# Hybrid RWKV-7 / NSA decoder step: the compression stage takes the prompt's group first, with its rows loaded in the stage ahead

## The chip, the cores and the metric

One core of one Trainium2 chip runs the whole kernel. The metric is device time in microseconds (us), median of several executions. All matrix work of the stage around the change is in fp32; each fp32 product shows as two PE instructions in the trace.

## The reference, cut to what matters

One inference step of one layer, for a prompt of 1024 tokens and 8 sample sequences of 4 new tokens with 2048 past tokens each. The NSA half compresses keys and values: a convolution of width 32 and stride 16 over the tokens, a bias from a position table, gelu, and a second product.

```
def _compress(x, w1, pe, w2):
    b, n, g, dh = x.shape
    xt = jnp.swapaxes(x, 1, 2).reshape(b * g, n, dh)
    h = lax.conv_general_dilated(xt, w1, (CMP_STRIDE,), 'VALID', dimension_numbers=('NWC', 'WIO', 'NWC'))
    h = jax.nn.gelu(h + jnp.einsum('rd,rdh->h', pe, w1)) @ w2
    return jnp.swapaxes(h.reshape(b, g, h.shape[1], dh), 1, 2)
```

It is called for keys and values of the prompt (kc, vc: columns of the projection of this step, 2 heads of 64) and of the samples (paged pools kc, vc with 2048 past tokens; the page table names the pages). The compressed keys are normalised over their 64 numbers.

## The kernel before, in words

The kernel is a row of stages, each an `nc.Block()`: the engines run their own instruction lists, semaphores order them, and all engines meet at a block's end. The first stages are `norm_in`, `project_nsa`, `compress`, `attend_prompt` and `attend_samples`; then come the RWKV half, merge, output projection and the two halves of the feed-forward.

**`project_nsa`.** Nine tiles of tokens (eight of 128, the last of 32), each multiplied into 1304 columns in three PSUM pieces by products of split operands (`split_product`, L173 to L175). ScalarE copies the result to `P`, VectorE normalises it (L532 to L548), PE turns it (L459 to L462), and SP stores the tile's kc, vc, ks, vs (and window) columns to DRAM (L409, L412, L414). SP's list also holds the loads of the adaLN weights, `ada(m)` (L385), one for each tile; PE multiplies them in `conditioned` (L182) after the tile's three pieces. At the head of the list stand two small loads (L379, L380) and two copies of window buffers from DRAM to DRAM (L383), then `ada(0)`. The last tile's stores are followed by a wait for all stores, and this ends the stage.

**`compress`.** Ten jobs, `JOBS = [(kind, grp) ...]`: five groups by two kinds (keys, values). Groups 0 to 3 are two sample sequences each, from 32 pages per group; group 4 (`PROMPT`) is the prompt. A job is `hidden(j)` (32 products of `w1` with 256 columns of pages, or with 64 columns of the prompt, two PE instructions each, L700), then gelu on ScalarE and VectorE (L751 to L756, L813 to L821), then `output(j)` (the product with `w2`, L713). For keys, `norm_keys` (L829 to L836) and `turn` (L723) follow. PE's order is hidden(j), turn of job j-2, output(j-1), so that gelu of a job lies under the next job's products.

The pages go to `X` (tile cx), which has two slots. SP and GpSimd load 16 pages each of every group (`load_pages`, L586: a register load of the page's number, then a 128 KB DMA). Groups 0 and 1 are loaded without a wait, groups 2 and 3 when the group two before has been multiplied (`conv`). When group 3 has been loaded and group 2 multiplied, SP loads the prompt's kc and vc rows back from DRAM (L657, four loads of 256 KB) into slot 0; PE turns them 8 blocks at a time through one PSUM tile (L686, pX), and ScalarE copies each set of 8 back (L745). The lines that order this on PE are

```
                        pe.wait_ge(xp_in[kind], 32)
                        for g in range(2):
                            if kind or g:
                                pe.wait_ge(xp_done, 2 * kind + g)
...
                        pe.wait_ge(xp_done, 2 * kind + 2)
```

The stage begins, on SP, with the page table, then `w1`, the position column and `w2` of each kind and a norm row (L645 to L650). PE waits for all seven (`w_in`), and computes the bias as 32 products of `w1` with one column (L669, two instructions each); the group 0 products follow when its pages are there.

Of the kernel before, what the change touches and what calls it, by code (L numbers as in the profile page):

```python
# [28 lines left out]
NB = 8  # L29
# [309 lines left out]
def project_nsa(nc, A, S, main, O, gate_dram):  # L339

    with ExitStack() as ctx:
# [247 lines left out]
def compress(nc, A, S, main, O, nsa):  # L589
# [4 lines left out]
    S["ckT"] = nsa.enter_context(nc.sbuf_tensor("ckT", [128, 9, 128], F32))  # L594
    S["cv"] = nsa.enter_context(nc.sbuf_tensor("cv", [128, 9, 128], F32))
    S["table"] = nsa.enter_context(nc.sbuf_tensor("table", [1, NB * PAGES], I32))
    with ExitStack() as ctx:
# [3 lines left out]
        X = sb("cx", [128, 2, 32, 2, 128])  # L601
        w1 = sb("cw1", [128, 2, 16, 128])
        pe_col = sb("cpe", [128, 2, 16])
        w2 = sb("cw2", [128, 2, 64])
        kn = sb("ckn", [128, 256])
        bias = sb("cbias", [128, 2])
# [9 lines left out]
        pB = ps("pB", [128, 2])  # L616
        pX = ps("pX", [128, 8, 64])
        w_in, tab_in = sem("cmp_w_in"), sem("table_in")
        x_in = [[sem(f"cmp_x{b}_{q}") for q in range(2)] for b in range(2)]
        xp_in = [sem("cmp_xp0"), sem("cmp_xp1")]  # L620
        conv, half, summed, squared, gate, gelu, proj, outc, ssum, root, knorm, turned, bias_mm, bias_done, xp_t, xp_done, kdone, chain = (
            sem(f"cmp_{n}") for n in ("conv", "half", "summed", "squared", "gate", "gelu", "proj", "out", "ssum", "root",
                                     "knorm", "turned", "bias_mm", "bias", "xp_t", "xp_done", "kdone", "chain"))

        PROMPT = 4
        JOBS = [(kind, grp) for grp in range(5) for kind in range(2)]
        n_of = lambda grp: (2, 128) if grp < PROMPT else (1, 64)
        flat = lambda b: X[:, b].rearrange("p a k c -> p (a k c)")
        raw_prompt = lambda b, kind: flat(b)[0:64, 2048 + 2048 * kind:4096 + 2048 * kind]
        turned_prompt = lambda b, kind: flat(b)[:, 1024 * kind:1024 * kind + 1024]  # L630
# [11 lines left out]
        with nc.Block() as block:  # L642
            @block.sync
            def _(sp):
                sp.dma_start(S["table"][:, :], A["page_table"]).then_inc(tab_in, 16)  # L645
                for k, n in enumerate("kv"):
                    sp.dma_start(w1[:, k], A[f"cw1_{n}"]).then_inc(w_in, 16)
                    sp.dma_start(pe_col[:, k], A[f"cpe_{n}"]).then_inc(w_in, 16)
# [3 lines left out]
                sp.wait_ge(conv, 2 * (PROMPT - 1))  # L652
                for kind in range(2):
                    src = (O["kc"], O["vc"])[kind][0].rearrange("(m r) c -> m r c", r=16)
                    for g in range(2):
                        dst = raw_prompt(PROMPT % 2, kind)[:, 1024 * g:1024 * g + 1024]
                        sp.dma_start(dst.rearrange("m (r d) -> m r d", d=HD),  # L657
                                     src[:, :, 64 * g:64 * g + 64]).then_inc(xp_in[kind], 16)
# [6 lines left out]
            def _(pe):  # L665
                pe.wait_ge(w_in, 16 * 7)
                for k in range(2):
                    for i in range(16):
                        mm = nc.tensor.matmul(pB[:, k:k + 1], w1[:, k, i, :], pe_col[:, k, i:i + 1],  # L669
                                              start=(i == 0), stop=(i == 15))  # L670
                mm.then_inc(bias_mm, 1)
                def hidden(j):
                    kind, grp = JOBS[j]
                    ns, nm = n_of(grp)
                    slot = grp % 2
                    if grp < PROMPT:
                        for q in range(2):
                            pe.wait_ge(x_in[slot][q], 16 * PAGES * (grp // 2 + 1))
                    else:

                        pe.wait_ge(xp_in[kind], 32)
                        for g in range(2):
                            if kind or g:
                                pe.wait_ge(xp_done, 2 * kind + g)
                            for i in range(8):
                                mm = nc.tensor.transpose(pX[:, i, :], raw_prompt(slot, kind)[:, 1024 * g + 128 * i:1024 * g + 128 * i + 128],  # L686
                                                         S["ident"][0:64, 0:64])
                            mm.then_inc(xp_t, 1)
                        pe.wait_ge(xp_done, 2 * kind + 2)
# [3 lines left out]
                    for g in range(2):  # L693
                        for hf in range(2):
                            for i in range(8):
                                if grp < PROMPT:
                                    rhs = X[:, slot, :, kind, 64 * g + 8 * i:64 * g + 8 * i + 8]
                                else:
                                    rhs = turned_prompt(slot, kind)[:, 512 * g + 64 * i:512 * g + 64 * i + 64]
                                mm = nc.tensor.matmul(pH[:, j % 2, g, hf, 0:ns * nm], w1[:, kind, 8 * hf + i, :], rhs,  # L700
# [34 lines left out]
            def _(act):  # L735
                act.wait_ge(bias_mm, 1)
                nc.scalar.activation(bias[:, :], pB[:, :], ACT.Copy).then_inc(bias_done, 1)
                act.wait_ge(bias_done, 1)
                def hidden(j):
                    kind, grp = JOBS[j]  # L740
                    ns, nm = n_of(grp)
                    if grp == PROMPT:
                        for g in range(2):
                            act.wait_ge(xp_t, 2 * kind + g + 1)
                            nc.scalar.activation(turned_prompt(grp % 2, kind)[:, 512 * g:512 * g + 512],  # L745
                                                 pX[:, :, :].rearrange("p i m -> p (i m)"), ACT.Copy).then_inc(xp_done, 1)
                    act.wait_ge(conv, j + 1)
# [10 lines left out]
                def keys_turned(grp):  # L758
                    ns, nm = n_of(grp)
                    seq = slice(2 * grp, 2 * grp + 2) if grp < PROMPT else slice(8, 9)  # L760
# [3 lines left out]
                def output(j):  # L764
                    kind, grp = JOBS[j]
                    ns, nm = n_of(grp)
                    seq = slice(2 * grp, 2 * grp + 2) if grp < PROMPT else slice(8, 9)
# [22 lines left out]
            def _(dve):  # L790
# [7 lines left out]
                dve.wait_ge(w_in, 16 * 7)  # L798
                link(nc.vector.memset(H[:, :, :], 0.0))

# [2352 lines left out]
def step_kernel(nc, A, OUT):  # L3153

    with ExitStack() as main:
# [18 lines left out]
        with mixes:  # L3174
            S["ybT"] = sb("ybT", [128, 4, T], mixes)
            with ExitStack() as nsa:
# [5 lines left out]
                S["gates"] = sb("gates", [128, 9, 24], nsa)  # L3182
                with ExitStack() as proj:
                    S["wn"] = [proj.enter_context(nc.sbuf_tensor(f"wn_{n}", [128, KC, NSA], F32R)) for n in ("hi", "lo")]
                    norm_in(nc, A, S, main)
                    project_nsa(nc, A, S, main, OUT, gate_dram)
                compress(nc, A, S, main, OUT, nsa)
# [112 lines left out]
```

## Time and profile before

| | |
|---|---|
| median of 3 runs | 2708.49 us (2705.33 to 2717.8) |
| the profiled execution: its time, its span | 2707.71 us, 2706.0 us |
| mean granted TensorE clock | 0.937 of full |
| PE busy | 2448.3 us, 90% of the span |
| `compress` stage | from 257.50 us to 449.0 us of the span |

The span is the time between the first and the last instruction of the profiled execution; a further 1.7 us lie around it. Times in the rows are us from the span's start. The granted clock is the share of full TensorE speed: 0.50 is 1.2 GHz, 1.00 is 2.4 GHz.

### The profile page before, as it was taken

The numbers are of one execution on the slowest core, as the hardware profiler recorded it, in microseconds if no ns is written. First come the engines' busy times: TensorE is split into PE (matmuls) and PEld (weight loads), VectorE is DVE, ScalarE is ACT, GpSimd is POOL, SyncE is SP. The second block draws the span as 40 slices with busy tenths as digits, with TensorE's granted clock in tenths as the row PEclk, the third lists the DMA queues.
The fourth block names the chain that finished last, engine by engine and source line by source line (L and its number), as shares of the span: only waits on it lengthen the run. The fifth ranks groups of instructions, "written<-read, shape, count | busy, mean of one in ns | idle before, by whom it ended". The sixth has DMA issues, their size and how long they took to land. (4 is left out here: it accounts for less than half of the span.)

```text
span 2706.0 us, 46990 instructions
## 1 busy us (share of the span) xinstructions
PE 2448.3 (90%) x19687; PEld 2067.5 (76%) x19687; DVE 1190.2 (44%) x2279; ACT 768.0 (28%) x1402; POOL 463.0 (17%) x348
## 2 busy tenths in 40 slices
PE   4796997999966889898999899999999999989998
PEld 2575886454533576676858799988899999989998
DVE  5242123555542153544535444456533333345665
ACT  3232122566620232213222332322111111113332
POOL 3000310000011000000000233351233333323332
PEclk7898895999976999999999799999999999999999
DMA  7433531101134100000000111133211111122221
GB/s 273 170 145 105 162 79 44 32 1 48 32 98 161 32 10 14 17 7 24 8 8 3 41 48 47 47 99 110 62 47 47 47 47 43 45 66 65 79 79 45
DMA packets 157972, 171.66 MB, mean 63 GB/s; under 512 B 14617, under 2 KB 143962, under 8 KB 155522
## 3 DMA queue, kind: packets, MB, share of 16 engines
q1 hardware_dynamic: 152130, 152.93, 18.0%
q0 software_dynamic: 5632, 15.74, 2.0%
q8 instruction: 156, 2.56, 0.4%
q14 instruction: 54, 0.44, 0.1%
HBM read 155.74 MB, written 17.05 MB: 64 GB/s over the span
## 5 line engine op out<-in xcount | busy, mean ns | idle before, releaser
L165 POOL CAST w_hi<-w_raw 128x1024 fp32r<-128x1024 f32 x102 | 108.2, 1061 | 1461.8 <-DMA w_raw<-in_w_in 671.6
L173 PE MATMUL pP_u<-h_hi,w_hi 128*128 128x352 f32 x1056 | 340.9, 323 | 0.3 <-PEq L2699 0.3
L174 PE MATMUL pP_u<-h_lo,w_hi 128*128 128x352 f32 x1056 | 338.5, 321 | 0.0
L175 PE MATMUL pP_u<-h_hi,w_lo 128*128 128x352 f32 x1056 | 338.3, 320 | 0.0
L167 POOL TENSOR_TENSOR w_lo<-w_raw,w_hi 128x1024 fp32r<-128x1024 f32 x102 | 243.2, 2385 | 8.2
L173 PEld LDWEIGHTS pP_u<-h_hi,w_hi 128*128 128x128 f32 x1056 | 198.1, 188 | 0.7 <-issue 0.6
L174 PEld LDWEIGHTS pP_u<-h_lo,w_hi 128*128 128x128 f32 x1056 | 198.5, 188 | 0.0
L175 PEld LDWEIGHTS pP_u<-h_hi,w_lo 128*128 128x128 f32 x1056 | 197.9, 187 | 0.0
L1659 PE MATMUL pB_e<-hT,w_rwkv 128*128 128x352 f32 x576 | 180.7, 470 | 16.7 <-DVE rw_slots L1683 9.5
L2988 DVE TENSOR_TENSOR conv<-conv,conv_sig 128x1056 f32<-128x1056 f32 x22 | 50.1, 2278 | 312.7 <-ACT conv_sig L2956 312.7
L173 PE MATMUL pP_d<-a_piece_hi,w_hi 128*128 128x352 f32 x528 | 173.8, 329 | 14.6 <-DVE a_piece_lo L3145 14.4
L3145 DVE TENSOR_TENSOR a_piece_lo<-aT,a_piece_hi 128x1408 fp32r<-128x1408 f32 (+1 forms) x72 | 139.3, 1941 | 97.1 <-ACT a_piece_hi L3081 97.1
L1659 PEld LDWEIGHTS pB_e<-hT,w_rwkv 128*128 128x128 f32 x576 | 109.7, 194 | 80.3 <-issue 25.8
L175 PE MATMUL pP_d<-a_piece_hi,w_lo 128*128 128x352 f32 x528 | 169.9, 322 | 0.0
L174 PE MATMUL pP_d<-a_piece_lo,w_hi 128*128 128x352 f32 x528 | 169.9, 322 | 0.0
L700 PE MATMUL pH<-cx,cw 128*128 128x256 f32 (+1 forms) x640 | 141.9, 392 | 1.5 <-ACT cx L745 1.4
L3081 ACT ACTIVATE a_piece_hi<-aT 128x1408 fp32r<-128x1408 f32 (+1 forms) x72 | 92.2, 1284 | 168.5 <-PE pP_d L175 163.4
L700 PEld LDWEIGHTS pH<-cx,cw 128*128 128x128 f32 x640 | 125.6, 221 | 15.4 <-ACT cx L745 1.7
L173 PE MATMUL pG_m<-h_hi,w_hi 128*128 128x352 f32 x384 | 125.2, 326 | 3.8 <-DVE h_lo L2648 3.8
L2075 PE MATMUL pB_rc<-rw_slots 64*64 64x64 f32 x3632 | 117.8, 220 | 11.5 <-DVE rw_slots L2436 8.1
L2075 PEld LDWEIGHTS pB_rc<-rw_slots 64*64 64x64 f32 x3632 | 110.7, 135 | 18.4 <-DVE rw_slots L2436 8.6
L174 PE MATMUL pG_m<-h_lo,w_hi 128*128 128x352 f32 x384 | 124.2, 323 | 0.0
(489 smaller groups left out, 4837.4 us busy)
## 6 DMA issues: line engine op xcount, KB each, us to landing
w_raw<-in_w_up SPq DMA_DIRECT2D x44, 512.0 KB, 4.2
ybT<-in_w_ada SPq DMA_DIRECT2D x9, 2048.0 KB, 7.6
kv_ring<-in_pool_kv SPq DMA_DIRECT2D x80, 128.0 KB, 2.1
w_raw<-in_w_down SPq DMA_DIRECT2D x20, 512.0 KB, 3.5
xt<-in_x SPq DMA_DIRECT2D x16, 512.0 KB, 4.7
cx<-in_pool_c POOLq DMA_DIRECT2D x64, 128.0 KB, 3.0
cx<-in_pool_c SPq DMA_DIRECT2D x64, 128.0 KB, 3.0
w_raw<-in_w_in SPq DMA_DIRECT2D x16, 512.0 KB, 4.2
```

The source lines that it names most:

```text
L165: engine.tensor_copy(hi, source).then_inc(done, 1)
L167: engine.tensor_tensor(lo, source, hi.bitcast(F32), ALU.subtract).then_inc(done, 1)
L173: nc.tensor.matmul(out, w_hi, x_hi, start=start, stop=False)
L174: nc.tensor.matmul(out, w_hi, x_lo, start=False, stop=False)
L175: return nc.tensor.matmul(out, w_lo, x_hi, start=False, stop=stop)
L700: mm = nc.tensor.matmul(pH[:, j % 2, g, hf, 0:ns * nm], w1[:, kind, 8 * hf + i, :], rhs, start=(i == 0), stop=(i == 7))
L1659: mm = nc.tensor.matmul(out[:, i, 0:PIECE], R["W"][:, n % 2, q, :], S["hT"][:, q, i * PIECE:(i + 1) * PIECE], start=(q == 0), stop=(q == K ...
L2075: mm = nc.tensor.matmul(dst[hr[h], c - 8 * g, :], lhs(hr[h], c), rhs(hr[h], c), start=True, stop=True)
L2988: link(nc.vector.tensor_tensor(c[:, :], c[:, :], sg[:, :], ALU.mult))
L3081: nc.scalar.activation(AR[0][:, m % 3, 0:b - a, :], aT[:, a:b, PIECE * i:PIECE * i + PIECE], ACT.Copy).then_inc(hi_done, 1)
L3145: nc.vector.tensor_tensor(AR[1][:, m % 3, 0:b - a, :], aT[:, a:b, PIECE * i:PIECE * i + PIECE], AR[0][:, m % 3, 0:b - a, :].bitcast(F32), ...
```

## The change

The prompt's group becomes group 0 of the ten jobs, and the four groups of pages follow as 1 to 4.

- `project_nsa`'s SP list loads the position columns (`cpe`) at its head, `w1` of the keys (`cw1_k`) after the last tile's products, and the prompt's kc and vc rows behind the last tile's norms, ahead of the last tile's stores. The projection's weights are in memory that `cx` and `cw1_k` now share, which is why these loads wait for `mm_done` 9.
- `compress` opens with the prompt's transposes, through two PSUM tiles instead of one, and waits for the weights of the values only ahead of the second job.
- The 32 bias products and their evictions go. VectorE writes two columns of the position table beside the prompt's 64 columns; the prompt's products have 66 columns, and the bias is the sum of column 64 of the first half and column 65 of the second, by two small ScalarE instructions in each prompt job.
- Pages: the group in slot 0 is loaded at once; the other three wait for `conv` 2, 4 and 6 (the rows and turned rows of the prompt lie in slot 1).

```
+                for k, n in enumerate("kv"):
+                    sp.dma_start(S["cpe"][:, k], A[f"cpe_{n}"]).then_inc(S["cmp_pe"], 16)
                 for m in range(2):
                     src = (A["win_k"], A["win_v"])[m]
...
+                    if i == 8:
+                        sp.wait_ge(mm_done, 9)
+                        sp.dma_start(S["cw1"][0][:, :, :], A["cw1_k"]).then_inc(S["cmp_k"], 16)
                     sp.wait_ge(copied, 4 * (i + 1))
                     sp.wait_ge(normed, i + 1)
+                    if i == 8:
+                        for q in range(2):
+                            sp.wait_ge(out_done[q], 16 * sum(n_out(i) for i in range(q, 8, 2)))
+                        for kind in range(2):
+                            src = (O["kc"], O["vc"])[kind][0].rearrange("(m r) c -> m r c", r=16)
+                            for g in range(2):
+                                dst = raw_prompt(S, kind)[:, 1024 * g:1024 * g + 1024]
+                                sp.dma_start(dst.rearrange("m (r d) -> m r d", d=HD),
+                                             src[:, :, 64 * g:64 * g + 64]).then_inc(S[f"cmp_xp{kind}"], 16)
...
+def raw_prompt(S, kind):
+    x = 2112 + 2048 * kind
+    return S["cx"][:, 1].rearrange("p a k c -> p (a k c)")[0:64, x:x + 2048]
+
+def turned_prompt(S, kind):
+    x = S["cx"][:, 1].rearrange("p a k c -> p (a k c)")[:, 1056 * kind:1056 * kind + 1056]
+    return x.rearrange("p (g i m) -> p g i m", g=2, i=8)
...
-        PROMPT = 4
+        PROMPT = 0
         JOBS = [(kind, grp) for grp in range(5) for kind in range(2)]
...
-            for grp in range(PROMPT):
-                if grp >= 2:
-                    eng.wait_ge(conv, 2 * (grp - 1))
+            for grp in range(4):
+                if grp:
+                    eng.wait_ge(conv, 2 * grp)
...
                 sp.dma_start(S["table"][:, :], A["page_table"]).then_inc(tab_in, 16)
+                sp.dma_start(w1[1][:, :, :], A["cw1_v"]).then_inc(w_in, 16)
                 for k, n in enumerate("kv"):
-                    sp.dma_start(w1[:, k], A[f"cw1_{n}"]).then_inc(w_in, 16)
-                    sp.dma_start(pe_col[:, k], A[f"cpe_{n}"]).then_inc(w_in, 16)
                     sp.dma_start(w2[:, k], A[f"cw2_{n}"]).then_inc(w_in, 16)
                 sp.dma_start(kn[:, :], A["norm_rows"]).then_inc(w_in, 16)
                 pages(sp, 0)
-                sp.wait_ge(conv, 2 * (PROMPT - 1))
...
-                pe.wait_ge(w_in, 16 * 7)
-                for k in range(2):
-                    for i in range(16):
-                        mm = nc.tensor.matmul(pB[:, k:k + 1], w1[:, k, i, :], pe_col[:, k, i:i + 1],
-                                              start=(i == 0), stop=(i == 15))
-                mm.then_inc(bias_mm, 1)
+                for kind in range(2):
+                    pe.wait_ge(xp_in[kind], 32)
+                    for g in range(2):
+                        if kind:
+                            pe.wait_ge(xp_done, g + 1)
+                        for i in range(8):
+                            mm = nc.tensor.transpose(pX[:, g, i, :], raw_prompt(S, kind)[:, 1024 * g + 128 * i:1024 * g + 128 * i + 128],
+                                                     S["ident"][0:64, 0:64])
+                        mm.then_inc(xp_t, 1)
+                pe.wait_ge(S["cmp_k"], 16)
+                pe.wait_ge(pe_ok, 4)
...
+                    cols = 66 if grp == PROMPT else 256
+                    if kind == 1 and grp == PROMPT:
+                        pe.wait_ge(w_in, 16 * 4)
...
-                                mm = nc.tensor.matmul(pH[:, j % 2, g, hf, 0:ns * nm], w1[:, kind, 8 * hf + i, :], rhs,
+                                mm = nc.tensor.matmul(pH[:, j % 2, g, hf, 0:cols], w1[kind][:, 8 * hf + i, :], rhs,
...
                     if grp == PROMPT:
+                        nc.scalar.activation(bias_half[:, kind:kind + 1], pH[:, j % 2, 0, 0, 64:65], ACT.Copy).then_inc(bias_one, 1)
+                        act.wait_ge(bias_one, kind + 1)
+                        nc.scalar.activation(bias[:, kind:kind + 1], pH[:, j % 2, 0, 1, 65:66], ACT.Identity,
+                                             bias=bias_half[:, kind:kind + 1]).then_inc(bias_done, 1)
...
+                dve.wait_ge(S["cmp_pe"], 32)
+                for kind in range(2):
+                    for g in range(2):
+                        nc.vector.tensor_copy(turned_prompt(S, kind)[:, g, :, 64:66],
+                                              pe_col[:, kind, :].rearrange("p (h i) -> p i h", h=2)).then_inc(pe_ok, 1)
                 link(nc.vector.memset(H[:, :, :], 0.0))
+                dve.wait_ge(w_in, 16 * 4)
```

## Rows read from the trace of the kernel before

**Rows 1.** Page, part 1: busy time, share of the span, instructions.

```profile
PE 2448.3 (90%) x19687; PEld 2067.5 (76%) x19687; DVE 1190.2 (44%) x2279; ACT 768.0 (28%) x1402; POOL 463.0 (17%) x348
```

**Rows 2.** Timeline, start of compress: start us, us, engine line op, [idle before].

```profile
252.71 0.33 SPq L409 DMA_DIRECT2D out_kc_s<-Pn  x1
...
255.24 0.68 SPq L414 DMA_DIRECT2D out_vw_s<-Pn  x1
257.50 0.26 SPq L645 DMA_DIRECT2D table<-in_page_table  x1
...
268.05 13.82 PE L669 MATMUL pB<-cpe,cw 128*128 128x1 f32 x64 [14.51 <-DMA ckn<-in_norm_rows]
...
277.78 0.54 POOL L586 DMA_DIRECT2D cx<-in_pool_c  x1 [0.61 <-issue]
```

**Rows 3.** Timeline of PE alone, page jobs (the first two, and a third).

```profile
282.00 29.89 PE L700 MATMUL pH<-cx,cw 128*128 128x256 f32 x128
...
312.56 14.03 PE L700 MATMUL pH<-cx,cw 128*128 128x256 f32 x64
```

**Rows 4.** Timeline, end of compress: last page job's output to the next stage.

```profile
400.59 0.99 PE L713 MATMUL p<-cw,cu 128*127 128x64 f32 x8
...
407.41 1.11 PE L686 MATMUL pX<-cst,cx 64*128 64x64 f32 x8 [5.18 <-ACT cx L745]
407.57 0.42 DVE L836 TENSOR_TENSOR ck_raw<-ck_raw,ckn 127x256 f32<-127x256 f32 x1
408.56 0.60 ACT L745 ACTIVATE cx<-pX 128x512 f32<-128x512 f32 x1 [1.20 <-PE pX L686]
...
409.21 13.92 PE L700 MATMUL pH<-cx,cw 128*128 128x64 f32 x64 [0.69 <-ACT cx L745]
...
423.34 1.81 PE L713 MATMUL p<-cw,cu 128*127 128x64 f32 x8
...
428.68 13.92 PE L700 MATMUL pH<-cx,cw 128*128 128x64 f32 x64 [0.69 <-ACT cx L745]
...
442.53 0.69 PE L713 MATMUL p<-cw,cu 128*63 128x64 f32 x4
...
447.74 0.69 PE L713 MATMUL p<-cw,cu 128*63 128x64 f32 x4
...
449.01 0.93 PEld L994 LDWEIGHTS ps_p<-ckT,qT 64*128 64x128 f32 x6 [0.78 <-issue]
```

**Rows 5.** Windows: us, busy of PE, PEld, DVE, ACT, POOL, granted clock, DMA share, GB/s.

```profile
268.00:275.00 7.00, 6.95 (x33) 6.95 (x33) 0.48 (x1) 0.00 (x0) 3.22 (x6) 0.50 0.95 309
...
282.00:285.00 3.00, 3.00 (x7) 2.46 (x8) 0.00 (x0) 0.08 (x1) 1.41 (x3) 0.50 0.71 225
285.00:290.00 5.00, 5.00 (x22) 4.27 (x22) 0.00 (x0) 0.00 (x0) 2.35 (x5) 0.89 0.81 236
...
409.00:416.00 7.00, 6.79 (x32) 6.79 (x33) 0.00 (x0) 0.15 (x1) 0.00 (x0) 0.50 0.01 2
```

**Rows 6.** Timeline of SP: the four loads of the prompt's rows.

```profile
371.17 1.34 SPq L657 DMA_DIRECT2D cx<-out_kc_p  x2
372.55 2.06 SPq L657 DMA_DIRECT2D cx<-out_vc_p  x2
```

**Rows 7.** Windows, the end of those loads; columns as in Rows 5.

```profile
378.00:379.00 1.00, 1.00 (x7) 0.87 (x6) 0.38 (x1) 0.00 (x0) 0.00 (x0) 1.00 1.09 123
379.00:379.50 0.50, 0.50 (x4) 0.45 (x3) 0.00 (x0) 0.00 (x0) 0.00 (x0) 1.00 0.07 6
```

**Rows 8.** Timeline, start of project_nsa: first adaLN weights, issue and use.

```profile
71.69 0.44 SPq L385 DMA_DIRECT2D ybT<-in_w_ada  x1
...
99.51 3.64 PE L182 MATMUL pM<-ybT,cT 128*32 128x512 f32 x16 [9.20 <-DMA ybT<-in_w_ada]
```

**Rows 9.** Timeline of SP: issues of a refill of 16 pages, group 2.

```profile
312.63 17.19 SPq L586 DMA_DIRECT2D cx<-in_pool_c  x16
```

**Rows 10.** Page, part 6: DMA issues, KB each, median us to landing.

```profile
cx<-in_pool_c POOLq DMA_DIRECT2D x64, 128.0 KB, 3.0
```

More of the change, by code:

```diff
@@ L600, in compress @@
         sem = lambda n: main.enter_context(nc.semaphore(n))
-        X = sb("cx", [128, 2, 32, 2, 128])
-        w1 = sb("cw1", [128, 2, 16, 128])
-        pe_col = sb("cpe", [128, 2, 16])
+        X, pe_col = S["cx"], S["cpe"]
+        w1 = S["cw1"] + [sb("cw1_v", [128, 16, 128])]
         w2 = sb("cw2", [128, 2, 64])
         kn = sb("ckn", [128, 256])
-        bias = sb("cbias", [128, 2])
+        bias, bias_half = sb("cbias", [128, 2]), sb("cbias_half", [128, 2])
         H2 = sb("ch2", [128, 2, 256])
@@ L615, in compress @@
         pT = ps("pTc", [128, 4, 128])
-        pB = ps("pB", [128, 2])
-        pX = ps("pX", [128, 8, 64])
+        pX = ps("pX", [128, 2, 8, 64])
         w_in, tab_in = sem("cmp_w_in"), sem("table_in")
         x_in = [[sem(f"cmp_x{b}_{q}") for q in range(2)] for b in range(2)]
[L620 to L623, printed above, removed]
-        PROMPT = 4
+        xp_in = [S["cmp_xp0"], S["cmp_xp1"]]
+        pe_ok, conv, half, summed, squared, gate, gelu, proj, outc, ssum, root, knorm, turned, bias_one, bias_done, xp_t, xp_done, kdone, chain = (
+            sem(f"cmp_{n}") for n in ("pe_ok", "conv", "half", "summed", "squared", "gate", "gelu", "proj", "out", "ssum", "root",
+                                     "knorm", "turned", "bias_one", "bias", "xp_t", "xp_done", "kdone", "chain"))
+        PROMPT = 0
         JOBS = [(kind, grp) for grp in range(5) for kind in range(2)]
[L627 to L630, printed above, removed]
+        n_of = lambda grp: (1, 64) if grp == PROMPT else (2, 128)
+        seq_of = lambda grp: slice(8, 9) if grp == PROMPT else slice(2 * grp - 2, 2 * grp)
         def pages(eng, queue):
             eng.wait_ge(tab_in, 16)
-            for grp in range(PROMPT):
-                if grp >= 2:
-                    eng.wait_ge(conv, 2 * (grp - 1))
+            for grp in range(4):
+                if grp:
+                    eng.wait_ge(conv, 2 * grp)
                 for q in range(queue, 2 * PAGES, 2):
@@ L674, in hidden @@
                     ns, nm = n_of(grp)
-                    slot = grp % 2
-                    if grp < PROMPT:
-                        for q in range(2):
[L678 to L689, printed above, removed]
+                    slot = (grp + 1) % 2
+                    cols = 66 if grp == PROMPT else 256
+                    if kind == 1 and grp == PROMPT:
+                        pe.wait_ge(w_in, 16 * 4)
+                    if grp == PROMPT:
+                        pe.wait_ge(xp_done, 2 * kind + 2)
+                    else:
+                        for q in range(2):
+                            pe.wait_ge(x_in[slot][q], 16 * PAGES * ((grp - 1) // 2 + 1))
                     if j >= 2:
@@ L735, in _ @@
             def _(act):
-                act.wait_ge(bias_mm, 1)
-                nc.scalar.activation(bias[:, :], pB[:, :], ACT.Copy).then_inc(bias_done, 1)
-                act.wait_ge(bias_done, 1)
+                for kind in range(2):
+                    for g in range(2):
+                        act.wait_ge(xp_t, 2 * kind + g + 1)
+                        nc.scalar.activation(turned_prompt(S, kind)[:, g, :, 0:64], pX[:, g], ACT.Copy).then_inc(xp_done, 1)
                 def hidden(j):
@@ L741, in hidden @@
                     ns, nm = n_of(grp)
+                    act.wait_ge(conv, j + 1)
                     if grp == PROMPT:
[L743 to L747, printed above, removed]
+                        nc.scalar.activation(bias_half[:, kind:kind + 1], pH[:, j % 2, 0, 0, 64:65], ACT.Copy).then_inc(bias_one, 1)
+                        act.wait_ge(bias_one, kind + 1)
+                        nc.scalar.activation(bias[:, kind:kind + 1], pH[:, j % 2, 0, 1, 65:66], ACT.Identity,
+                                             bias=bias_half[:, kind:kind + 1]).then_inc(bias_done, 1)
+                        act.wait_ge(bias_done, kind + 1)
                     if j:
@@ L796, in link @@
                     dve.wait_ge(chain, count[0])
-                dve.wait_ge(w_in, 16 * 7)
+                dve.wait_ge(S["cmp_pe"], 32)
+                for kind in range(2):
+                    for g in range(2):
+                        nc.vector.tensor_copy(turned_prompt(S, kind)[:, g, :, 64:66],
+                                              pe_col[:, kind, :].rearrange("p (h i) -> p i h", h=2)).then_inc(pe_ok, 1)
                 link(nc.vector.memset(H[:, :, :], 0.0))
+                dve.wait_ge(w_in, 16 * 4)
                 def gelu_of(j):
@@ L3185, in step_kernel @@
                     norm_in(nc, A, S, main)
+                S["ckT"] = sb("ckT", [128, 9, 128], nsa)
+                S["cv"] = sb("cv", [128, 9, 128], nsa)
+                S["table"] = nsa.enter_context(nc.sbuf_tensor("table", [1, NB * PAGES], I32))
+                with ExitStack() as pages:
+                    S["cx"] = sb("cx", [128, 2, 32, 2, 128], pages)
+                    S["cw1"] = [sb("cw1_k", [128, 16, 128], pages)]
+                    for n in ("cmp_k", "cmp_pe", "cmp_xp0", "cmp_xp1"):
+                        S[n] = main.enter_context(nc.semaphore(n))
                     project_nsa(nc, A, S, main, OUT, gate_dram)
-                compress(nc, A, S, main, OUT, nsa)
+                    compress(nc, A, S, main, OUT)
                 S["kv_ring"] = sb("kv_ring", [128, 4, PAGES, 256], nsa)
```

22 lines of the change are left out of this document (7 added, 15 removed).

## The prediction, made before the result was known

> **What bounds the kernel now.** I began with the busy shares [rows 1]: PE is busy for 90% of the span, so the kernel is a PE kernel, and a change is worth what it takes out of PE's idle time or out of PE's work at a low clock. The chain that ended last lies in the feed-forward and says nothing of this stage, so I took the timeline at the stage's two ends. At the start [rows 2], the projection's last stores are issued from 252.71 to 255.92, the stage begins at 257.50, and PE stands until 268.05, when the last of seven loads has landed. It then does the bias (13.8 us) and starts on pages at 282.00 [rows 3]. The reader should see that the bias is not what PE would otherwise do without: GpSimd issues the sixteenth and last page of the first group at 277.78 [rows 2], 0.54 us later it is out, and with 3.0 us to landing [rows 10] that is 281.3. The bias lies in the shadow of the pages. Taking it away alone would be worth under 1 us; what matters is that something useful takes its place.
>
> From 282.00 to 400.59 PE does eight page jobs without a gap [rows 3, 4], 118.6 us. After that comes what is dear: the prompt's rows are turned through one PSUM tile with ScalarE between, and the first prompt job starts at 409.21, 8.6 us after the last page product; the second at 428.68, 5.6 us after the first's end at about 423.1; its last product ends at 442.53, and the next stage begins at 449.01 [rows 4].
>
> The windows tell the third thing [rows 5]. In the bias, and in the prompt's jobs, PE is busy for 6.8 to 7 of 7 us, yet the granted clock is 0.50 (1.2 GHz). Under page products, with 256 columns, it is 0.50 at 282 to 285 and 0.89 over 285 to 290: it rises. So 64 instructions take 13.85 us in a prompt job (428.68 to 442.53) with 64 columns, the same 13.82 us with one column [rows 2], and 14.03 us with 256 columns at full clock [rows 3]. At 1 and at 64 columns the time is that of loading the weights (PEld is as busy as PE in both), so 66 columns should cost what 64 do.
>
> **The change part by part.** I set the new stage beside the old one, in us of the span.
>
> *Two position loads at the head of the projection.* This is not free. PE waits 9.20 us for the first adaLN weights, which land at 99.51 though issued at 71.69 [rows 8]. An issue takes 0.44 us there, so two more in front put that load, and the large copies ahead of it, later by some 0.9 us, and PE with it. Bounds: nothing if the landing is set by the copies' own bytes, 2 us if the small packets hold the queue as well. I take +0.9.
>
> *Loads ahead of the last stores.* The key weights go out behind the last products, ahead of SP's wait for the last tile's norms, so that load lies under VectorE's norm work and is wanted only by the first job. Then four loads of the prompt's rows stand in front of six stores. SP took 371.17 to 374.61 to issue them, 3.44 us [rows 6]. The stores and the stage's end move by that: 257.50 becomes 260.9. Bounds: nothing less than 3.0, and 5 if the stores' data wait behind the rows' data. All four had landed by about 379.1 [rows 7], 7.9 us from the first issue; from 252.7 that is 260.6, just in time for the new stage's first PE instruction at 260.9.
>
> *Transposes first.* Four sets of eight at 1.11 us [rows 4] (half clock) are 4.4 us. With two PSUM tiles the third set waits only for ScalarE's 0.60 us copy of the first, which lies under the second. VectorE's four small copies of the position columns lie beside them. First job at 265.3.
>
> *Prompt jobs.* 2 x 13.85 = 27.7, with job 0's output of 0.69 [rows 4] behind: to 293.7. The value weights are wanted at 279.2, 18 us into the stage; before, all seven loads were there 10.5 us into it. The two extra ScalarE instructions follow the products and delay only gelu, which lies under the next job; without cover they would cost, each at most a copy's 0.60, about 1 us in a job.
>
> *Pages.* GpSimd's sixteenth page was issued 20.3 us after the stage's start [rows 2]; now 281.2, landed at 284.7, 9 us ahead of need. The next group, which used to come at once, now waits for `conv` 2 at 293.0. A refill is issued in 17.2 us and lands 3.0 us later [rows 9, 10], with GpSimd about a microsecond behind SP some 21.5 us in all; a pair of page jobs covers 29.7. All three refills have 8 us to spare, as the two of before had. Behind SP's and GpSimd's waits stands nothing but further pages. Page phase 118.6 us as before, so to 412.3. Its first pair held 1.8 us of half clock (29.89 against 2 x 14.03 [rows 3]); I keep it, with 0 as the other end.
>
> *Tail.* The stage now ends with a page group. From its last product (like 400.59) the key norm runs to 407.99 [rows 4]; then the transposes, about 0.4, the output in its large form at the low clock, 1.81, and copy and handover, 449.01 less 448.43, 0.6. That is 10.2 us, against 6.5 for the small group (442.53 to 449.01). The end is at 422.5. Bounds 9 to 11.
>
> The sum: 449.0 - 422.5 = 26.5, less 0.9 at the projection's head, is 25.6 us. Seen from the other side: the 41.9 us between last page product and last prompt product (400.59 to 442.53), of which 14.2 were gaps, are gone; the 24.5 us ahead of the first page product become 36.2 (3.4 of stores, 4.4 of transposes, 28.4 of prompt jobs), which costs 11.7; the tail costs 3.7. Against the profiled execution's own 2707.71 (span 2706.0, 1.7 around it) this gives 2682.1. That execution lies 0.8 below the median of the runs shown, so I say 2682.
>
> **Rule and row: the clock.** The rows show the clock at 0.50 through 13.8 us of bias products and again through both prompt jobs, with PE all but fully busy. The Trainium skill ("TensorE: Matmul & The Clock Gate", section "What's actually happening") says that sustained activity releases the throttle. By that rule the prompt jobs would run fast; the trace here disagrees, and the sum goes by the trace. The same page's rule fits the page products, which do rise.
>
> **Rivals.**
>
> *B, the prompt jobs at full clock.* They now follow each other without the old gap, 27.7 us on end with two columns more. If the clock rises in them, the price is that of narrow products at full clock: 0.99 us for eight against 1.81 at half [rows 4], a factor 0.55. Two jobs save 12.5 us, the page phase's 1.8 goes as well: 2668. For it: the longer unbroken stretch. Against: three such stretches stayed at 0.50. Chance 0.08.
>
> *C, the prompt's rows land late.* They have 0.3 us to spare by my count. Each piece is 64 numbers, 256 B; they moved at 123 GB/s near their end, with the queues full [rows 7]; here the stores come on top. Twice the time is 268.5, and all behind it is later by 7.6: 2690. The Trainium skill ("DMA: Bandwidth & Descriptors") says that pieces under 512 B do not run at line rate, and the trace agrees with that 123 GB/s. Chance 0.09.
>
> *D, slower.* The page products start behind 32 us of work at half clock; if that kept the clock from rising, each microsecond at half clock would lose half a microsecond. Over the whole page phase, eight jobs of 14.03 more, that is 112 us, 2794; from some 51 us at half clock on, the change loses. Against it: at 282 the clock was at half after the bias and rose within the first pair [rows 5]. Chance 0.03.
>
> *E, no change.* The refills come short: the group that used to be in place now has to arrive in 29.7 us. Beyond its 8 us of slack each refill's lateness is paid, three times over. Refills of 38 us instead of 21.5 would bring 2707. The old refills, of the same size and cover, did not stop PE between the rows at 282.00 and 400.59. Chance 0.03.
>
> **How the numbers follow.** The forecast has the remaining 0.77, with its own range of 2677 to 2688 from the bounds above and the spread of the runs. To leave out no more than 2 in 10, the range takes in B and C: 2667 to 2692. 0.5% (13.5 us) is about what a measurement of this kernel can tell from no change. A, B and C are all faster by more: 0.94 less a little for a C worse than twice, 0.93; within 0.5% 0.04; slower 0.03.
>
> **What the changed profile would show.** Stage start near 262 (with the 0.9 from the head), first prompt product about 5 us after it at clock 0.50; two jobs of 13.8 us; no PE gap until the tail; first page product near 295; next stage near 423.5. I am wrong if PE's wait at the stage's start names the prompt's rows, if the clock in the prompt jobs is 1.00, if a page product waits for `cx`, or if the later stages, which should only move, change their length.

## The result

The changed kernel takes 2683.38 us (median of 4, 2682.48 to 2687.05), the kernel before 2708.38: ratio 0.9908, 95% interval 0.9891 to 0.9925, 25.0 us less. A control, the same changed kernel measured again among later runs, gave 2687.49 (6 runs, 2681.4 to 2692.1) against 2710.32, ratio 0.992 (0.9904 to 0.9936). So the gain is 23 to 25 us. The forecast was 2682 and a gain of 25.6.

The page of the changed kernel, part 1, against [rows 1]:

```profile
PE 2437.7 (91%) x19623; PEld 2056.4 (77%) x19623; DVE 1191.3 (44%) x2283; ACT 768.7 (29%) x1405; POOL 462.9 (17%) x348
```

PE has lost 64 instructions, which are the bias products, and only 10.6 us of busy time. The rest of the 20.6 us between the two spans (2706.0 and 2685.4) is idle time. In the lines of a timeline, the brackets say how long the engine was idle before, and what ended it; SPq and PEq are the instruction queues of SP and PE. The timeline of the changed kernel at the stage's start, against [rows 2, 6]:

```profile
252.07 1.34 SPq L419 DMA_DIRECT2D cx<-out_kc_p  x2
...
253.45 2.27 SPq L419 DMA_DIRECT2D cx<-out_vc_p  x2
255.76 1.61 SPq L423 DMA_DIRECT2D out_kc_s<-Pn  x1
257.41 0.42 SPq L423 DMA_DIRECT2D out_vc_s<-Pn  x1
...
259.59 0.71 SPq L428 DMA_DIRECT2D out_vw_s<-Pn  x1
262.51 0.26 SPq L664 DMA_DIRECT2D table<-in_page_table  x1
```

The four loads hold SP for 3.7 us. The first store then takes 1.61 us to issue instead of 0.33, and after the last store's issue (260.30) it is 2.2 us to the next stage, not 1.6. From the first issue to the stage's start it was 4.79 us (252.71 to 257.50), now it is 10.44 (252.07 to 262.51).

PE alone, in the changed kernel, against [rows 3, 4]:

```profile
262.55 3.81 PE L683 MATMUL pX<-cst,cx 64*128 64x64 f32 x32 [9.65 <-PEq L376]
266.28 13.92 PE L711 MATMUL pH<-cx,cw_k 128*128 128x66 f32 x64
279.99 13.86 PE L711 MATMUL pH<-cx,cw_v 128*128 128x66 f32 x64
293.79 0.69 PE L724 MATMUL p<-cw,cu 128*63 128x64 f32 x4
294.40 16.13 PE L711 MATMUL pH<-cx,cw_k 128*128 128x256 f32 x64
...
413.82 0.99 PE L724 MATMUL p<-cw,cu 128*127 128x64 f32 x8
421.29 0.69 PE L734 MATMUL pTc<-cst,ck_raw 127*128 127x127 f32 x2 [6.47 <-DVE ck_raw L855]
421.77 1.81 PE L724 MATMUL p<-cw,cu 128*127 128x64 f32 x8
424.31 1.08 PE L1013 MATMUL ps_p<-ckT,qT 64*128 64x63 f32 x6 [0.73 <-PEq L661]
```

No line between 262.55 and 413.82 has a bracket: PE waits for nothing there. Its one wait is the stage's start itself (PEq), and the last is the key norm of the tail. The windows of the changed kernel, with columns as in [rows 5]:

```profile
267.00:274.00 7.00, 7.00 (x34) 7.00 (x34) 0.00 (x0) 0.00 (x0) 3.01 (x7) 0.50 0.89 271
...
288.00:294.00 6.00, 6.00 (x30) 5.88 (x30) 0.00 (x0) 0.11 (x1) 0.00 (x0) 0.50 0.00 0
...
297.00:298.00 1.00, 1.00 (x4) 0.73 (x4) 0.35 (x2) 1.00 (x1) 0.54 (x1) 0.50 0.74 206
298.00:299.00 1.00, 1.00 (x5) 0.86 (x4) 0.58 (x3) 0.31 (x2) 0.52 (x1) 0.71 0.69 229
299.00:310.00 11.00, 11.00 (x53) 9.68 (x52) 0.15 (x1) 0.00 (x0) 4.86 (x10) 1.00 0.82 230
```

The clock is at 0.50 (1.2 GHz) through both prompt jobs, 27.5 us of unbroken PE work (266.28 to 293.79), and rises some 4 us into the page products.

From the first SP issue behind the last norms to the next stage's first PE work, before took 196.3 us (252.71 to 449.01), after 172.2 (252.07 to 424.31): 24.1 less. The profiled pair differs by only 20.7 us as a whole (2707.71 and 2687.05), and the changed kernel's profiled execution is the slowest of its four. The missing 4 us lie in the RWKV stage, from its first pB_e product to merge's first: 618.8 us in the profile of before (903.8 to 1522.6), 622.8 after. This is one of the signs of being wrong that the prediction named, a later stage that changes its length. The other traces speak against the change as its cause: the two later kernels with the old order have 622.0 and 623.1, the last kernel below, with the new order, 618.7, and the remaining eight lie between 621.5 and 622.9. So it differs between executions under either order.

### The profile page after: what moved, and what is told of

It reads as the page before. It is cut to its first block and busy times, and to the rows that moved or that the text cites. A ratio compares the mean times of both kernels' runs of the same rounds, so it can differ in the third digit from the quotient of the medians.

```text
span 2685.4 us, 46871 instructions
## 1 busy us (share of the span) xinstructions
PE 2437.7 (91%) x19623; PEld 2056.4 (77%) x19623; DVE 1191.3 (44%) x2283; ACT 768.7 (29%) x1405; POOL 462.9 (17%) x348
## 5 line engine op out<-in xcount | busy, mean ns | idle before, releaser
L173 PE MATMUL pP_d<-a_piece_hi,w_hi 128*128 128x352 f32 x528 | 173.8, 329 | 14.4 <-DVE a_piece_lo L3164 14.3
L2094 PE MATMUL pB_rc<-rw_slots 64*64 64x64 f32 x3632 | 119.3, 221 | 12.2 <-DVE rw_slots L2455 8.1
L175 PE MATMUL pG_m<-h_hi,w_lo 128*128 128x352 f32 x384 | 124.1, 323 | 0.0
L1102 DVE CUSTOM_DVE_ANT_0 kv_ring<-ps_p,dist_p 128x320 f32<-128x320 f32 (+5 forms) x192 | 93.1, 521 | 62.6 <-PE ps_p L1013 61.8
```

Of the source, the lines that this page charges most:

```text
L173: nc.tensor.matmul(out, w_hi, x_hi, start=start, stop=False)
L175: return nc.tensor.matmul(out, w_lo, x_hi, start=False, stop=stop)
L1102: nc.vector.tensor_tensor_reduce(held(n)[:, 4 * g + j, at], pS[:, k % 3, 0:w], table(n)[:, at], 1.0, -3e38, ALU.add, ALU.max, tops[:, n % ...
L2094: mm = nc.tensor.matmul(dst[hr[h], c - 8 * g, :], lhs(hr[h], c), rhs(hr[h], c), start=True, stop=True)
```

## The experiments

Each time is a median; the kernel before, on the same chips, took 2709.4 to 2710.3. "Stage" is from the compress stage's start to the next stage's first product: 191.5 us before, 161.8 after. "First issue" is SP's first issue behind the last tile's norms.

### The bias products left out of the old order

```
-                for k in range(2):
-                    for i in range(16):
-                        mm = nc.tensor.matmul(pB[:, k:k + 1], w1[:, k, i, :], pe_col[:, k, i:i + 1],
...
+                nc.vector.memset(bias[:, :], 0.0).then_inc(bias_done, 1)
```

> The kernel before, in its old order, with the 32 bias products left out (the bias is then zero: the position table's part is missing from the result). My theory, the bias lies in the shadow of the first pages: PE starts on pages at about 281.5 of the span instead of 282.0, and the time falls by no more than 1 us, 2708. Rival, the gain of the change is the bias work taken away: the time falls by 13 us or so, to 2695, with the first page product at 268.

Measured: 2709.59, ratio 1.0 (0.9986 to 1.0014). PE alone in that kernel:

```profile
282.90 30.82 PE L695 MATMUL pH<-cx,cw 128*128 128x256 f32 x128 [28.54 <-DMA cx<-in_pool_c]
```

All of the 13.8 us turned into a wait for pages: 28.54 us instead of 14.51 for the weights. The first page product comes 24.6 us after the stage's start (258.32), as before (24.5). The removal alone is worth nothing.

### The bias products put back into the new order

```
                     if kind == 1 and grp == PROMPT:
                         pe.wait_ge(w_in, 16 * 4)
+                        for k in range(2):
+                            for i in range(16):
+                                nc.tensor.matmul(pT[:, k, 0:1], w1[k][:, i, :], pe_col[:, k, i:i + 1],
```

> The changed kernel with the 32 bias products put back between the first and the second prompt job, their result unused. My theory: in the new order nothing hides them, since PE has no wait left there, so they cost their whole 13.8 us at half clock: 2697. Rival, they are hidden in this order too (PE would wait for pages otherwise): under 2 us, 2684 to 2685.

Measured: 2700.96 (10 runs, 2695.37 to 2710.78), ratio 0.9967 (0.9953 to 0.998); stage 175.2 us, 13.4 more than the changed kernel's. The time is 13.5 us above the control's. PE alone:

```profile
266.82 13.92 PE L715 MATMUL pH<-cx,cw_k 128*128 128x66 f32 x64
280.54 6.93 PE L698 MATMUL pTc<-cpe,cw_k 128*128 128x1 f32 x32
287.32 6.96 PE L698 MATMUL pTc<-cpe,cw_v 128*128 128x1 f32 x32
294.15 13.90 PE L715 MATMUL pH<-cx,cw_v 128*128 128x66 f32 x64
```

The same products that were free in the old order cost their full length in the new one. The two columns of bias and the new order belong together: once the prompt's work fills the time in which pages arrive, nothing is left to hide the bias. Of the 24 us at the next stage's start, 13.4 hang on the two columns.

### The prompt's rows loaded at the compress stage's head

```
-                                sp.dma_start(dst.rearrange("m (r d) -> m r d", d=HD),
-                                             src[:, :, 64 * g:64 * g + 64]).then_inc(S[f"cmp_xp{kind}"], 16)
                     for (op, os), c in outs:
...
                 sp.dma_start(S["table"][:, :], A["page_table"]).then_inc(tab_in, 16)
+                for kind in range(2):
+                    src = (O["kc"], O["vc"])[kind][0].rearrange("(m r) c -> m r c", r=16)
+                    for g in range(2):
...
+                        sp.dma_start(dst.rearrange("m (r d) -> m r d", d=HD),
+                                     src[:, :, 64 * g:64 * g + 64]).then_inc(S[f"cmp_xp{kind}"], 16)
                 sp.dma_start(w1[1][:, :, :], A["cw1_v"]).then_inc(w_in, 16)
```

> The changed kernel with the four loads of the prompt's rows moved from the projection's SP list to the head of the compress stage, behind the page table. My theory: the early load is worth little, because it holds up the stage's end by as much as it saves. Stage start 5.6 us earlier (about 4.8 us after the first of the last stores), rows landed 8 to 9 us after that, first prompt product about 2 us later than in the changed kernel: 2685, not to be told from it by time, but by the trace. Rival, the early load is a main part of the gain: 8 us lost, 2691.

Measured: 2689.05, ratio 0.9915 (0.989 to 0.9939). PE alone:

```profile
263.15 1.96 PE L680 MATMUL pX<-cst,cx 64*128 64x64 f32 x16 [10.16 <-DMA cx<-out_kc_p]
267.00 1.96 PE L680 MATMUL pX<-cst,cx 64*128 64x64 f32 x16 [1.88 <-DMA cx<-out_vc_p]
268.89 13.92 PE L708 MATMUL pH<-cx,cw_k 128*128 128x66 f32 x64
```

The stage starts at 256.93, and PE waits for the rows. From the last norms' end (first SP issue, 252.17) the first prompt product is at 16.7 us, against 14.2 in the changed kernel. So the early load is worth 2.5 us of 24, near the 2 of the first theory. The time, above the 2685 expected, is 1.6 us above the control's and can't tell.

### The last stores ahead of the prompt's loads

```
                         if i == 8:
                             sp.dma_start(os[:, WIN - DS:WIN, :], P[0:n, i % 2, c:c + 128]).then_inc(out_done[i % 2], 16)
+                for q in range(2):
+                    sp.wait_ge(out_done[q], 16 * sum(n_out(i) for i in range(q, 8, 2)))
+                for kind in range(2):
+                    src = (O["kc"], O["vc"])[kind][0].rearrange("(m r) c -> m r c", r=16)
...
                 for q in range(2):
                     sp.wait_ge(out_done[q], 16 * sum(n_out(i) for i in range(q, 9, 2)))
```

> The changed kernel with the projection's last six stores ahead of the four loads of the prompt's rows, both still in the projection's list. My theory: the stores cost the 5.6 us of the stage's start because they queue behind the loads; in this order the stage starts about 7 us after the first store's issue (SP has still to issue the loads) instead of 10.4, but the rows land later by the same 3 us, so that the first prompt product comes within 1 us of where it was: 2683 to 2685. Rival, the late stage start is what costs: 3 us gained at the first product.

Measured: 2688.0, ratio 0.9918 (0.9901 to 0.9934). PE alone:

```profile
264.92 1.97 PE L682 MATMUL pX<-cst,cx 64*128 64x64 f32 x16 [8.34 <-DMA cx<-out_kc_p]
268.23 1.96 PE L682 MATMUL pX<-cst,cx 64*128 64x64 f32 x16 [1.34 <-DMA cx<-out_vc_p]
270.12 13.92 PE L710 MATMUL pH<-cx,cw_k 128*128 128x66 f32 x64
```

First issue 255.76, stage start 263.29 (7.5 us later instead of 10.4), first prompt product 270.12: 14.4 us after the first issue, against 14.2. What the stage's start gains, the rows' landing takes. The time is 0.5 us above the control's.

### Two PSUM tiles in the old order

```
-        pB = ps("pB", [128, 2])
-        pX = ps("pX", [128, 8, 64])
+        pB = pT[:, 0, 0:2]
+        pX = ps("pX", [128, 2, 8, 64])
```

The bias sums move into a corner of another PSUM tile (pT), to make room for the second one.

> The kernel before in its old order, with the prompt's transposes through two PSUM tiles instead of one. My theory, the gaps at the stage's end are ScalarE's: its copies of the turned rows queue behind gelu, the key copy and a table load of the page jobs, and a second tile takes away only the exchange between PE and ScalarE: 1.2 us before the first prompt job and about 1.8 before the second, 3 us, 2706. Rival, the single tile makes the 14 us of gaps, and the reordering was not needed: 2697.

Measured: 2710.81, ratio 0.9999 (0.9988 to 1.001). PE alone, from the last page job's output on:

```profile
403.76 0.99 PE L713 MATMUL p<-cw,cu 128*127 128x64 f32 x8
404.69 1.20 PE L686 MATMUL pX<-cst,cx 64*128 64x64 f32 x16
411.06 13.92 PE L700 MATMUL pH<-cx,cw 128*128 128x64 f32 x64 [5.17 <-ACT cx L745]
```

ScalarE in the same kernel:

```profile
407.53 0.63 ACT L756 ACTIVATE cu<-cu 128x512 f32<-128x512 f32 x1 [2.73 <-DVE cu L819]
408.06 0.37 ACT L772 ACTIVATE ck_raw<-p 127x256 f32<-127x256 f32 x1
408.45 1.28 ACT L776 ACT_TABLE_LOAD   x1
409.74 0.30 ACT L776 ACTIVATE cst_c<-cst_c,cst 127x4 f32<-127x4 f32 x1
409.95 1.06 ACT L745 ACTIVATE cx<-pX 128x512 f32<-128x512 f32 x2
```

The transposes are done at 405.9, their copies start at 409.95, behind gelu, the key copy, a table load and a root. The first prompt product comes 7.3 us after the last page product instead of 8.6. The second tile takes away about 1.3 us there and 0.9 before the second job, less than the 3 expected and not to be measured in the time. The first gap was made by where the prompt's group stood in ScalarE's queue. In the second, PE itself is busy with the turning of keys, an output and the transposes (424.77 to 428.9), and waits only 0.69 us.

### Both heads in one product of 132 columns

```
+                    if grp == PROMPT:
+                        for hf in range(2):
+                            for i in range(8):
+                                mm = nc.tensor.matmul(both(j, hf), w1[kind][:, 8 * hf + i, :], turned_prompt(S, kind)[:, :, i, :],
```

> The changed kernel with both heads' columns in one product of 132 columns, so a prompt job has 16 products instead of 32 of 66. My theory, a prompt job costs its weight loads: 32 instructions of about 0.22 us at half clock, 7.0 us instead of 13.8, and the time falls by 13.6 us to 2670; if the wider products also bring full clock, by up to 4 us more. Rival, the job is bound by columns passed through the array: the same time, 2683.

Measured: 2679.14, ratio 0.9883 (0.9859 to 0.9907). PE alone:

```profile
265.42 6.38 PE L715 MATMUL pH<-cx,cw_k 128*128 128x132 f32 x32
271.64 3.76 PE L715 MATMUL pH<-cx,cw_v 128*128 128x132 f32 x32
275.33 0.44 PE L734 MATMUL p<-cw,cu 128*63 128x64 f32 x4
285.17 16.98 PE L721 MATMUL pH<-cx,cw_k 128*128 128x256 f32 x64 [9.40 <-DMA cx<-in_pool_c]
```

Windows of the same kernel:

```profile
269.00:270.00 1.00, 1.00 (x7) 1.00 (x6) 0.00 (x0) 0.00 (x0) 0.54 (x1) 0.50 0.98 234
270.00:271.00 1.00, 1.00 (x8) 1.00 (x8) 0.00 (x0) 0.00 (x0) 0.54 (x1) 0.70 0.83 261
271.00:272.00 1.00, 1.00 (x12) 1.00 (x11) 0.00 (x0) 0.16 (x1) 0.54 (x1) 1.00 0.89 230
```

The two jobs take 9.9 us instead of 27.5. That is more than half gone, more than the merging alone gives, because the clock rises inside the first. But 9.4 us come back as a wait for pages, a bound I had not named in the expectation: the first group lands 23.5 us after the stage's start, here and in the next kernel. In the wait the clock falls, and the first page job takes 16.98 us. A net 7.5 us of the stage is gained (154.3), and the time is 9 us above the 2670 expected.

### As many products as before, each with 132 columns

```
-                                    rhs = turned_prompt(S, kind)[:, g, i, :]
+                                    rhs = turned_prompt(S, kind)[:, :, i, :]
```

> The changed kernel with as many products as it has in the prompt jobs, but each with both heads' columns (132), half of which nobody reads. Twice the columns for the same weight loads. My theory, drawn from the merged run: the clock in the prompt jobs depends on what the products stream, and rises some 5 us into the first job; from there an instruction takes about 0.11 us instead of 0.22. The two jobs take about 17 us instead of 27.4, and PE then waits for pages as the merged kernel did: first page product at about 23.5 us after the stage's start, 2679. Rival, the clock stays at 0.50 and the jobs take 28.2 us: 2684.

Measured: 2677.81, ratio 0.9891 (0.9874 to 0.9907). PE alone:

```profile
264.20 9.72 PE L720 MATMUL pH<-cx,cw_k 128*128 128x132 f32 x64
273.76 7.36 PE L720 MATMUL pH<-cx,cw_v 128*128 128x132 f32 x64
...
283.87 14.05 PE L720 MATMUL pH<-cx,cw_k 128*128 128x256 f32 x64 [2.37 <-DMA cx<-in_pool_c]
```

Windows of the same kernel:

```profile
262.00:266.00 4.00, 4.00 (x28) 3.80 (x28) 0.00 (x0) 1.99 (x4) 1.72 (x3) 0.50 0.88 334
266.00:270.00 4.00, 4.00 (x25) 4.00 (x25) 0.00 (x0) 0.00 (x0) 1.66 (x4) 0.64 0.88 255
270.00:271.00 1.00, 1.00 (x11) 1.00 (x11) 0.00 (x0) 0.00 (x0) 0.54 (x1) 1.00 0.86 236
...
276.00:283.00 7.00, 5.49 (x50) 5.23 (x48) 1.35 (x7) 1.54 (x6) 3.23 (x6) 1.00 0.73 219
283.00:286.00 3.00, 2.13 (x10) 1.93 (x11) 1.55 (x7) 2.05 (x4) 1.32 (x3) 1.00 0.81 215
```

Twice the columns through the array with the same number of weight loads, and the two jobs take 16.9 us instead of 27.5. Nor were the columns the limit at the low clock: in the first 4.0 us of the first job, still at 0.50, 19 instructions of 132 columns ran, against 20 of 66 columns in the changed kernel. That settles the merged kernel's rival too. PE waits 2.4 us for pages with the clock still at 1.00, and the first page job takes 14.05 us, where the changed kernel's took 16.13. So the stage takes 151.3 us, 3.0 less than the merged kernel's, although its prompt jobs have twice the instructions.

### The page table and 12 pages in the projection stage

```
+            @block.gpsimd
+            def _(pool):
+                pool.wait_ge(mm_done, 9)
+                pool.wait_ge(S["table_in"], 16)
+                for q in range(1, 24, 2):
+                    load_pages(nc, pool, S, A["pool_c"], q, S["cx"][:, 0, q].rearrange("p k c -> p (k c)"), S["x_in"][0][1])
```

> The merged kernel (132 columns, 16 products a job) with the page table and 12 of the first group's 32 pages loaded in the projection stage, behind its last products, by GpSimd; the other 20 are shared out 10 and 10 at the compress stage's start. My theory: the merged kernel lost its gain to the wait for these pages (9.4 us). They land now at about 15 to 17 us after the stage's start instead of 23.5, so the page jobs start at about 278 instead of 285: 2671 to 2673. Rival, the pages delay the prompt's rows and the last stores by as much as they gain: 2679.

Measured: 2670.32, ratio 0.9855 (0.9838 to 0.9871). PE alone:

```profile
264.87 3.81 PE L697 MATMUL pX<-cst,cx 64*128 64x64 f32 x32 [12.55 <-PEq L376]
...
280.59 14.08 PE L727 MATMUL pH<-cx,cw_k 128*128 128x256 f32 x64 [1.42 <-DMA cx<-in_pool_c]
```

The wait for pages is 1.4 us instead of 9.4, and the page jobs start at 280.6, not 278. The stage's start is later by 3 us than in the merged kernel (13.4 us behind the first issue instead of 10.4), so part of the rival was true too. The larger part of those 3 us is the wait behind the last store's issue, 4.8 us instead of 2.3. From the first issue to the next stage it is 157.0 us, against 164.7 in the merged kernel. Of the 7.7 us between them 2.9 are the clock's: it stays up through the short wait, and the first page job takes 14.08 us instead of 16.98.

### The first adaLN weights ahead of the window copies

```
+                def ada(m):
+                    sp.dma_start(wa, A["w_ada"][:, 4 + m]).then_inc(wa_in, 16)
...
+                ada(0)
+                gate_bias(0)
                 for k, n in enumerate("kv"):
                     sp.dma_start(S["cpe"][:, k], A[f"cpe_{n}"]).then_inc(S["cmp_pe"], 16)
...
-                ada(0)
-                gate_bias(0)
                 for i, (t0, n) in enumerate(TILES):
```

> The changed kernel with the first adaLN weight load (and its bias row) ahead of the position columns and the two window copies. My theory: PE's 9.6 us wait at about 99 us is that load standing behind the window copies' 4 MB; ahead of them it lands some 8 us after its issue, PE does not wait, and the clock does not fall there: 10 to 12 us gained, 2673. Rival, the wait only moves to the next load on that queue: 2681 to 2684.

Measured: 2674.49, ratio 0.9875 (0.9858 to 0.9891). PE alone:

```profile
88.47 1.93 PE L182 MATMUL pM<-ybT,cT 128*32 128x512 f32 x16
```

There is no bracket: the 9.6 us wait is gone, and the 16 instructions take 1.93 us instead of 3.64. None of the seven later loads of the kind is waited for either, so the rival is out. The compress stage starts 12.2 us earlier, counted from the projection's first SP issue (181.9 us against 194.0).

### All of it

The early pages and the adaLN load first, together, with the merged products.

> The kernel with early pages and merged prompt products, and the first adaLN load ahead of the window copies. If the two gains are of separate waits, they add: 2670.3 less the 9 us of the adaLN run, 2661. Rival, the window copies, now later, press on the rest: 2665 to 2668.

Measured: 2661.41 (2652.16 to 2666.98), ratio 0.9826 (0.9805 to 0.9847): 49 us below the kernel before, 22 to 26 below the changed one. PE at the next stage's start:

```profile
397.10 1.08 PE L1029 MATMUL ps_p<-ckT,qT 64*128 64x63 f32 x6 [0.73 <-PEq L676]
```

The two gains add. From the projection's first SP issue to this product it is 355.6 us in the control (67.36 to 422.96), 342.8 with the adaLN load first (67.56 to 410.40), 340.8 with early pages and merged products (67.65 to 408.45), and 328.4 with both (68.73 to 397.10). That is 12.8 and 14.8 us, together 27.6, and 27.2 measured.

### The changed kernel again

> The changed kernel again, unedited, as a control. All theories: 2683 to 2685; stage from its start to the next stage 161.8 us; the RWKV stage's length differs between executions by some us in either direction (in the profiled pair it took 5 us of the gain).

Measured: 2687.49, ratio 0.992 (0.9904 to 0.9936), 2.5 us above the expected range. Its stage took 161.6 us, its profiled execution had a span of 2679.7, and six runs spread over 11 us. Differences of 2 or 3 us between kernels are therefore read here from stages, not from medians.

## Why the prediction was right, point by point

| step | predicted | measured |
|---|---|---|
| two position loads ahead of the first adaLN load | +0.9 | +0.3 (first SP issue to first use: 30.32, now 30.66) |
| loads ahead of the last stores | +3.4 | +5.65 (4.79, now 10.44) |
| transposes | 4.4 | 3.7 |
| two prompt jobs and an output | 28.4 | 28.1 |
| page phase | 118.6 | 119.4 |
| tail | 10.2 | 10.5 |
| first SP issue to next stage | -26.5 | -24.1 |
| whole | -25.6 | -25.0 by the medians, -22.8 by the control |

**How close it was.** The mechanism was right, and the sum at the next stage's start was 2.4 us too good (26.5 forecast, 24.1 measured), nearly all of it in the stores. That the medians came within 1 us of the sum is luck: the control of the same kernel lies 4.1 us higher. One small slip of the sum: 2682.1 was for an execution 0.8 us below the median, so the median's own forecast was 2682.9, not 2682.

**The bound.** That the bias lay in the shadow of the pages is shown by leaving it out (nothing gained), and that folding it in is nevertheless needed by putting it back (13.4 us lost).

**The stores.** This term was mis-sized, by 2.2 us. I counted SP's 3.44 us of issuing and took nothing for the stores' place behind 1 MB of loads. The first store's issue grew by 1.3 us, the wait after the last by 0.6, and the loads themselves took 0.2 more to issue. The upper bound of 5 was passed as well. Swapping stores and loads showed that this costs nothing at the first product, because the rows' landing comes next. No wait for the rows shows, and rival C did not come about, but the late start helped. The last of the four loads was issued at 254.5 and took 6.6 us at most to land, so the rows were there by 261.1, 9.0 us behind the first issue and not 7.9 (9.8 where they were loaded in the stage, 9.2 behind the stores). The stage began 1.4 us after that; at the forecast 260.9 no margin would have been left.

**The clock.** At 66 columns it stayed at 0.50 for 27.5 us on end, as the rows of before said and against rival B. The rule of the Trainium skill that I set beside it ("TensorE: Matmul & The Clock Gate", section "What's actually happening") would have given a rise here, and the trace again disagrees. The factor 0.55 that priced B can be set only beside wider products: at full clock, an instruction of 132 columns took 0.12 us instead of the 0.22 of one of 66 at half clock (3.76 us for 32, 13.92 for 64). No run had 66 columns at full clock.

**The refills.** The group that now waits for the prompt jobs arrived in time, as did the others: no page product waits for `cx` in the changed kernel. Rivals D and E did not come about: the clock rose with the page products, and no refill was late. Pages that come later than PE wants them are real all the same, for the first group: the merged kernel met them at once.

**The position loads.** Smaller than taken, within the bounds. The adaLN load was issued 0.9 us later, as counted (3.43 us behind the first SP issue instead of 2.50), but its use only 0.3 later. This fits the lower bound, a landing set by the copies' own bytes; with the load ahead of the copies, the wait was gone. The larger fact was in the same row [rows 8]: the 9.2 us wait itself, which I used only to price 0.9 us.

**The tail, the transposes and the page phase** were right within 1 us. The first page job held 2.1 us of half clock (16.13 against 14.03) where I had kept the 1.8 of before.

What stays open is why the RWKV stage takes 619 us in some executions and 623 in others, and what makes the clock rise for products of 132 columns and not for those of 66. Neither was tried further.

## What to carry to other kernels

Work that is hidden has no price of its own until the order changes: the same 32 products cost nothing, or 13.4 us, by what stands beside them. When a group of work is odd (other source, other engine path), put it where the engines would wait anyway, and then ask at once what bounds that place next; here it was the first pages, 23.5 us after the stage's start. Look at loads that PE waits for at the head of a stage, and at what was put ahead of them in the same queue.

## What the runs showed of the hardware that I had not expected

- More columns took less time. With the weight loads unchanged (64 instructions a job), 66 columns ran at 0.50 of the clock and took 13.7 to 13.8 us a job; 132 columns reached 1.00 some 5 us into the first job and took 7.3 us in the second.
- A store's issue by SP took 1.61 us instead of 0.33 when it followed the four loads of 256 B pieces. It isn't about stores: where a load of weights came behind the same four, its issue took 1.60 us instead of 0.35.
- Through PE's wait of 2.4 us the clock stayed at full (the first page job behind it took 14.05 us); in the one of 9.4 us it fell to half (16.98 us).
